# Value projections of the last block with swapped PSUM banks, the short convolution's activation four slots further up, gate rows read out ahead of the splits

## What is computed

```python
def second_block(x, norm_pre, norm_post, w_in, b_if, conv_qk, lambda_qk, norm_a, norm_b, w_a, w_b, w_out):
    h = _rmsnorm(x, norm_pre[l])
    proj = jnp.einsum('bsd,dn->bsn', h, w_in[l])
    qa, ka, va, za, qb, kb, vb, ob, zb, igb, fgb, ga, gb = _split(proj, sizes)
    ...
    oa = _diff_attention(qa, ka, va, lam)
    oa = _rmsnorm(oa, norm_a[l].reshape(H_A, 2 * HEAD_DIM_A)) * (1.0 - lam_init)
    ya = oa.reshape(B, S, W_A) * jax.nn.silu(za)
    qk = jax.nn.silu(_causal_conv(jnp.concatenate([qb, kb], axis=-1), conv_qk[l]))
    ...
    hb = _mlstm(qb_c, kb_c, vb, ig, fg)
    hb = jax.nn.sigmoid(ob.astype(jnp.float32)).reshape(B, S, H_B, HEAD_DIM_B) * hb
    hb = _rmsnorm(hb, norm_b[l].reshape(H_B, HEAD_DIM_B)).astype(x.dtype)
    yb = hb.reshape(B, S, W_B) * jax.nn.silu(zb)
    merged = (jax.nn.sigmoid(ga) * jnp.einsum('bsw,wd->bsd', ya, w_a[l])
              + jax.nn.sigmoid(gb) * jnp.einsum('bsw,wd->bsd', yb, w_b[l]))
    out = jnp.einsum('bsd,de->bse', merged, w_out[l])
    x = x + _rmsnorm(out, norm_post[l])
```

## Time and profile before

| what | value |
|---|---|
| median of 3 executions | 1253.1 us (1253.06 to 1255.51) |
| the profiled execution's own time | 1250.83 us |
| its span, first to last instruction | 1249.6 us |
| TensorE matmul busy | 1220.2 us |
| TensorE weight load busy | 1069.8 us |
| VectorE busy | 881.7 us |
| ScalarE busy | 682.0 us |
| GpSimd busy | 60.7 us |
| granted TensorE clock, mean | 0.996 |
| DMA | 215.46 MB, mean 172 GB/s |

### The profile page before, as it was taken

How to read it: one execution, slowest core, us unless ns; L and a number is a source line. 1 busy time by engine, 2 the same in 40 slices (tenths; PEclk the granted TensorE clock), 3 DMA queues, 4 the chain that set the end, 5 groups by cost and what they waited for, 6 DMA issues and landing times.

```text
span 1249.6 us, 18894 instructions
## 1 busy us (share of the span) xinstructions
PE 1220.2 (98%) x7518; PEld 1069.8 (86%) x7518; DVE 881.7 (71%) x1255; ACT 682.0 (55%) x1033; POOL 60.7 (5%) x89
## 2 busy tenths in 40 slices
PE   7999999989999999999999999999999999899998
PEld 6888888867888888888888887988888899788996
DVE  6686856885787766777766667587776668565875
ACT  5655544533665555555654457556655445555463
POOL 4000100100010000000000122000000000000000
PEclk9999999999999999999999999999999999999999
DMA  8766566771566655666655555156665665646450
GB/s 273 233 206 188 165 189 192 205 183 42 164 195 184 195 172 177 194 192 189 192 183 163 176 190 165 35 152 197 191 194 177 184 188 169 174 118 156 144 174 34
DMA packets 205653, 215.46 MB, mean 172 GB/s; under 512 B 9808, under 2 KB 192592, under 8 KB 205566
## 3 DMA queue, kind: packets, MB, share of 16 engines
q1 hardware_dynamic: 202998, 210.76, 56.8%
q10 hardware_dynamic: 2568, 3.50, 0.9%
HBM read 212.19 MB, written 2.03 MB: 171 GB/s over the span
## 4 chain that ended last, share of the span: by engine, by line
PE 92%; ACT 3%; DVE 2%; issue 1%; DMA 0%; ACTq 0%; POOL 0%; SPq 0%
PE psum L504 90%; ACT whi L1295 1%; DVE wlo L1896 1%; PE psum L668 0%; DMA xn<-in_x 0%; PE psum L953 0%; ACT qn L1599 0%; PE psum L696 0%; ACT L1735 0%; ACTq L1410 0%; DVE small L2333 0%; DVE oa L2543 0%; PE psum L1108 0%; ACT qkc L1699 0%; PE psum L906 0%
## 5 line engine op out<-in xcount | busy, mean ns | idle before, releaser
L504 PE MATMUL psum<-x,whi 128*128 128x512 f32 (+1 forms) x2288 | 696.2, 365 | 5.3 <-ACT whi L1295 2.4
L1896 DVE TENSOR_TENSOR wlo<-raw,whi 128x1024 fp32r<-128x1024 f32 (+2 forms) x403 | 474.3, 1189 | 193.3 <-ACT whi L1295 190.0
L504 PE MATMUL psum<-x,wlo 128*128 128x256 f32 x1960 | 549.3, 280 | 0.8 <-DVE wlo L1896 0.8
L1295 ACT CAST whi<-raw 128x1024 fp32r<-128x1024 f32 (+2 forms) x403 | 406.2, 1022 | 171.6 <-PE psum L504 162.5
L504 PEld LDWEIGHTS psum<-x,whi 128*128 128x128 f32 x2288 | 409.4, 189 | 79.6 <-ACT whi L1295 2.8
L504 PEld LDWEIGHTS psum<-x,wlo 128*128 128x128 f32 x1960 | 371.3, 189 | 1.5 <-DVE wlo L1896 1.3
L504 PE MATMUL psum<-g,whi 128*128 128x512 f32 x704 | 247.7, 396 | 0.0
L504 PE MATMUL psum<-g,wlo 128*128 128x256 f32 x704 | 197.6, 281 | 0.0
L504 PEld LDWEIGHTS psum<-g,whi 128*128 128x128 f32 x704 | 132.3, 188 | 31.8
L504 PE MATMUL psum<-whi,x 128*128 128x512 f32 (+1 forms) x512 | 141.2, 376 | 4.7 <-ACT va L1768 3.3
L504 PEld LDWEIGHTS psum<-g,wlo 128*128 128x128 f32 x704 | 132.2, 188 | 0.0
(11 more groups left out here) (321 smaller groups left out, 851.1 us busy)
## 6 DMA issues: line engine op xcount, KB each, us to landing
raw<-in_ffn_w_gate SPq DMA_DIRECT2D x88, 512.0 KB, 4.5
raw<-in_ffn_w_up SPq DMA_DIRECT2D x88, 512.0 KB, 4.2
raw<-in_ffn_w_down SPq DMA_DIRECT2D x80, 512.0 KB, 3.8
raw<-in_w_in SPq DMA_DIRECT2D x52, 512.0 KB, 3.8
raw<-in_w_o SPq DMA_DIRECT2D x16, 512.0 KB, 4.7
raw<-in_a_w_in SPq DMA_DIRECT2D x14, 512.0 KB, 4.7
raw<-in_w_kv SPq DMA_DIRECT2D x16, 384.0 KB, 3.3
raw<-in_w_mem_kv SPq DMA_DIRECT2D x8, 512.0 KB, 3.7
```

Source lines behind the costliest of these rows:

```text
L504: return pe.matmul(o, l, r, start=start, stop=stop, skip_group_check=True)
L1295: act.copy(held(B.whi[:, i % SPLIT, :], *n), held(B.raw[:, i % RAW, :], *n)).then_inc(*s.hi.now(i))
L1896: dve.tensor_tensor(held(B.wlo[:, i % SPLIT, :], *n), held(B.raw[:, i % RAW, :], *n), held(B.whi[:, i % SPLIT, :], *n).bitcast(F32), ALU.s ...
```

## The change

Three parts, all in the last block.

1. `VB2` is computed into banks 6 and 7 and `VA2` into 4 and 5. TensorE's waits for the first z/o group and for the first transposes of the attention change places with them. On ScalarE the two activations of the short convolution and the one-element exponential stand right behind the read of `vb`, ahead of `use(VA2 + 1)` to `use(VA2 + 3)`, that is, ahead of the splits of z/o slots 1 to 3.
2. In `rest` on VectorE the read of a z/o group's bank 7 stands ahead of `use` in the fourth slot, not behind it.
3. For the third z/o group VectorE reads bank 6 as well; ScalarE's read of it is gone. TensorE's first two column blocks and `z_fn(2)` wait for VectorE.

```diff
@@ -437,7 +437,7 @@
     s.c_act = sig("mix_c_act", ["lam", "ln", ("qk", 0), ("qk", 1)])
     s.v_act = sig("v_rows_act", ["vb", "va"])
     s.ysq = sig("y_squares", [(k, j) for k in ("a", "b") for j in range(8)])
-    s.zo_act = sig("zo_act", range(3))
+    s.zo_act = sig("zo_act", range(2))
     s.z_fn = sig("zo_fn", [1, 0, 2])
     s.expF = sig("mlstm_floor", range(8))
     s.gab_act = sig("gab_sigmoid", range(4))
@@ -483,7 +483,8 @@
     s.cc = sig("conv4", range(4))
     s.c_dve = sig("mix_c_dve", ["g8", "lamsum", "gt", "gmin", "aqk0", "aqk1", "lf", "aqk2", "aqk3", "lam", "vb", "F", "w",
                                 "va", ("zz", 0), ("zz", 2)])
-    s.zo_dve = sig("zo_dve", range(3))
+
+    s.zo_dve = sig("zo_dve", range(4))
     s.gab = sig("gab_cols", range(16))
     s.wd = sig("mlstm_diag", range(8))
     s.floor = sig("mlstm_floor_in", range(8))
@@ -1085,10 +1086,8 @@
                 pe.wait_ge(*s.zo_dve.at(i - 1))
             yield from rows_steps((xh[0], xl[0]), None, 8, ZO2 + 4 * i, 512, [[6], [7]], first=i)
         for c in range(16):
-            if c == 0:
-                pe.wait_ge(*s.zo_act.at(2))
-            elif c == 1:
-                pe.wait_ge(*s.zo_dve.at(2))
+            if c < 2:
+                pe.wait_ge(*s.zo_dve.at(2 + c))
             else:
                 pe.wait_ge(*s.gab.at(c - 2))
             i = GAB2 + c
@@ -1164,13 +1163,13 @@
                 pair(0, 0, AQK2 + 2 * c + e, (6, 7, 2, 3)[c], range(4 * e, 4 * e + 4), e == 0, e == 1)
                 if c == 0 and e == 0:
                     gate_turn()
+        pe.wait_ge(*s.c_dve.at("aqk1"))
+        rows(X0, None, 8, VB2, 512, [[6], [7]])
+        pe.wait_ge(*s.qk.at(2))
+        decay_sums()
         pe.wait_ge(*s.row.at(6))
         pe.wait_ge(*s.c_dve.at("gt"))
-        rows(X0, None, 8, VB2, 512, [[4], [5]])
-        pe.wait_ge(*s.qk.at(2))
-        decay_sums()
-        pe.wait_ge(*s.c_dve.at("aqk1"))
-        rows(X0, None, 8, VA2, 512, [[6], [7]])
+        rows(X0, None, 8, VA2, 512, [[4], [5]])
         rg = rest()
         for i in range(10):
             if i < 8:
@@ -1179,13 +1178,14 @@
                 diff_scores(i)
             if 0 <= i - 1 < 8:
                 if i == 1:
-                    pe.wait_ge(*s.v_act.at("vb"))
+                    pe.wait_ge(*s.v_act.at("va"))
+                    pe.wait_ge(*s.c_dve.at("va"))
                 weights_turn2("d", i - 1)
             if 0 <= i - 2 < 8:
                 values2("d", i - 2, MC.va)
             if i == 0:
-                pe.wait_ge(*s.v_act.at("va"))
-                pe.wait_ge(*s.c_dve.at("va"))
+                pe.wait_ge(*s.v_act.at("vb"))
+                pe.wait_ge(*s.c_dve.at("vb"))
             next(rg)
         for _ in range(3):
             next(rg)
@@ -1703,7 +1703,7 @@
         for i in range(3):
             for k in range(4):
                 use(ZO2 + 4 * i + k)
-                if k == 3:
+                if k == 3 and i < 2:
                     act.wait_ge(*s.zo0.at(i))
                     act.activation(MC.zob[:, i, 0, :], bank[6], ACT.Copy, scale=small[:, 14:15]).then_inc(*s.zo_act.now(i))
                 yield
@@ -1729,8 +1729,9 @@
         act.copy(MC.ptbuf[:, i % 2, 0:nk * 128], bank[4][:, 0:nk * 128]).then_inc(*s.pt_act.now((st, i)))
 
     def z_fn(i, fn):
-        act.wait_ge(*s.zo_act.at(i))
-        act.wait_ge(*s.zo_dve.at(i))
+        if i < 2:
+            act.wait_ge(*s.zo_act.at(i))
+        act.wait_ge(*s.zo_dve.at(i if i < 2 else 3))
         z = flat(MC.zob[:, i])
         act.activation(z, z, fn).then_inc(*s.z_fn.now(i))
 
@@ -1758,14 +1759,14 @@
             use(VB2 + i)
         use(VA2)
         act.wait_ge(*s.used.at(VB2 + 3))
-        act.activation(MC.vb[:, 0, :], bank[4], ACT.Copy, scale=small[:, 14:15]).then_inc(*s.v_act.now("vb"))
-        for i in range(1, 4):
-            use(VA2 + i)
+        act.activation(MC.vb[:, 0, :], bank[6], ACT.Copy, scale=small[:, 14:15]).then_inc(*s.v_act.now("vb"))
         for h in range(2):
             silu_cols(h)
         act.activation(small[0:1, 319:320], B.ones[0:1, 0:1], ACT.Exp)
+        for i in range(1, 4):
+            use(VA2 + i)
         act.wait_ge(*s.used.at(VA2 + 3))
-        act.activation(MC.va[:, 0, :], bank[6], ACT.Copy, scale=small[:, 14:15]).then_inc(*s.v_act.now("va"))
+        act.activation(MC.va[:, 0, :], bank[4], ACT.Copy, scale=small[:, 14:15]).then_inc(*s.v_act.now("va"))
         rg = rest()
         for i in range(10):
             if i < 8:
@@ -2459,11 +2460,15 @@
     def rest():
         for i in range(3):
             for k in range(4):
-                use(ZO2 + 4 * i + k)
                 if k == 3:
+                    if i == 2:
+                        dve.wait_ge(*s.zo0.at(2))
+                        dve.tensor_scalar(MC.zob[:, 2, 0, :], bank[6], small[:, 14:15], None, ALU.mult).then_inc(
+                            *s.zo_dve.now(2))
                     dve.wait_ge(*s.used.at(ZO2 + 4 * i + 3))
                     dve.tensor_scalar(MC.zob[:, i, 1, :], bank[7], small[:, 15:16], None, ALU.mult).then_inc(
-                        *s.zo_dve.now(i))
+                        *s.zo_dve.now(i if i < 2 else 3))
+                use(ZO2 + 4 * i + k)
                 yield
         for c in range(16):
             use(GAB2 + c)
@@ -2615,7 +2620,7 @@
             some(cg, 2)
         some(cg, 100)
         dve.wait_ge(*s.used.at(VB2 + 3))
-        dve.tensor_scalar(MC.vb[:, 1, :], bank[5], small[:, 15:16], None, ALU.mult).then_inc(*s.c_dve.now("vb"))
+        dve.tensor_scalar(MC.vb[:, 1, :], bank[7], small[:, 15:16], None, ALU.mult).then_inc(*s.c_dve.now("vb"))
         use(VA2)
         dve.wait_ge(*s.pe_c.at("F"))
         dve.tensor_copy(Fc, in_pairs(bank[0][:, 0:8])).then_inc(*s.c_dve.now("F"))
@@ -2624,7 +2629,7 @@
         for i in range(1, 4):
             use(VA2 + i)
         dve.wait_ge(*s.used.at(VA2 + 3))
-        dve.tensor_scalar(MC.va[:, 1, :], bank[7], small[:, 15:16], None, ALU.mult).then_inc(*s.c_dve.now("va"))
+        dve.tensor_scalar(MC.va[:, 1, :], bank[5], small[:, 15:16], None, ALU.mult).then_inc(*s.c_dve.now("va"))
         rg = rest()
         dve.wait_ge(*s.c_dve.at("lam"))
         for i in range(10):
```

## The result

The changed kernel took a median of 1245.5 us in five executions (1244.4 to 1247.0), the kernel before 1253.1. The ratio is 0.9934, 95% interval 0.9921 to 0.9946: 8.3 us less by the ratio, with an interval of 6.8 to 9.9. The forecast was 1246.2. The profiled execution took 1244.4 with a span of 1242.9; forecast for its kind, against the profiled execution of before, were 1243.9 and 1242.7.

A forecast was written before the change was run, and what follows sets the result against it. TensorE was taken as the bound, busy 98% at full clock, so only its waits could give time. 3.42 + 0.38 + 1.02 + 2.10 = 6.9 us off the median 1253.1 gave 1246.2 us, range 1244.0 to 1250.0.

The forecast's parts named there:

- The first wait: TensorE between job 0's scores and the z/o rows, waiting for bank reads: z/o rows start 3.42 us earlier.
- The new wait at the turn of job 0: TensorE coming for job 0's weights: weights ready 1.2 us ahead of it, so no new wait there.
- The cover of the splits: ScalarE's splits of z/o slots 1 to 3 behind the moved activation: 6.8 us of delay before TensorE waits.
- The slower rival: Late splits of z/o slots 1 to 3 stop TensorE; 14 us delay for no change, 1256 us at 17; chance 0.03.
- The first group's end: TensorE's wait after the first group of z/o rows goes as VectorE reads bank 7 before its subtraction: 0.38 us.
- The second group's end: After the second group of z/o rows, VectorE's earlier read of bank 7 lets TensorE go on 1.02 us earlier.
- The third group: VectorE alone reads the third z/o group: first column block 2.2 us earlier, third column block 2.10 us earlier.
- Behind it: After the third column block the program is unchanged: nothing given back, nothing more gained.
- The sum: Whole gain in the last block: 3.42 + 0.38 + 1.02 + 2.10 = 6.9 us.
- The upper figure of 7.6: Top of the forecast gain, 7.6 us, if no remainder of TensorE's waits stays in the last block.
- The clock: TensorE's granted clock taken as full throughout the span, from the profile before the change.

The follow-up runs named there:

- the repeat: The changed kernel, unaltered, timed once more on the chip of two other runs: 1245.3 us, ratio 0.9926 (0.9913 to 0.9939) against the kernel before.

## Why the prediction was right, and where not

**The first wait.** Forecast 3.42, measured 3.44. The reason holds: ScalarE's queue, not the bank, carried nearly all of it. The text gave the whole of it to both edits together; apart, the move gains 3.05 and the swap alone 1.3, because the swap alone brings a wait of 1.45 us at the turn of job 0.

**The new wait at the turn of job 0.** Forecast: weights at about 1090.7, TensorE at 1091.85, lead 1.2. Measured: weights at 1090.58 (1090.23 + 0.35), TensorE at 1091.64, lead 1.06.

**The cover of the splits.** Forecast 6.8 us, measured 1.8. This is the step that failed, though it changed nothing in the time. The text priced the subtraction of z/o slot 1 alone; three of them stand in VectorE's queue ahead of the read of bank 5. The slower rival would have decided from 1.8 us of delay on and evened out the gain at 1.8 + 6.6 = 8.4 before the clock's part, not at 14. With the clock's part it was sooner: 6 us of delay gave 162.05 to the end, 0.7 more than before, and a median 1.4 us under that of before; 12 us gave a median 4 us over it.

The rule of the Trainium skill ("ScalarE: Activation LUTs", What ACT_TABLE_LOAD costs), 1.38 us of drain behind a table load, would have mattered here. By an estimate from that figure, two drains are 2.8 us, more than the cover of 1.8, and a wait of 1 us would have stood at job 0. The traces do not have the drain, and no wait stands there. In the runs with added loads a load and its one-element activation take 1.50 us, 1.28 of it the load, and in the changed kernel the activation starts 1.30 after its load did (1077.92, 1079.22).

**The first group's end.** Forecast 0.38, measured 3.97 - 3.44 = 0.53.

**The second group's end.** Forecast 1.02, measured 4.53 - 3.97 = 0.56. The order of read and subtraction did what it should. From job 7's transposes to slot 8 it took 2.09 us before (1123.50, 1125.59) and takes 1.02 now (1119.92, 1120.94), 1.07 less. But the transposes themselves, 3.97 ahead after the first group, are only 3.46 ahead: 0.51 us went there, 0.34 of it as a tag. The text had counted on TensorE coming to this turn with no wait. The round of a job over ScalarE and VectorE takes 4.4 us and starts no earlier than its own work allows; job 5's maxima came 3.1 us earlier, TensorE 4.0. Before, TensorE's waits at the group ends had kept that round ahead (by 0.5 us at job 7: weights at 1123.03, transpose at 1123.50). At the group's end itself it was then ScalarE's read of bank 6, behind its cast (1120.18 + 0.70), that ended last, and no longer VectorE's (1119.95 + 0.74). That a bound of the second rank lies half a microsecond behind the first was not looked for.

**The third group.** Forecast 2.2 at the first column block, 2.10 at the third. Measured 2.13 and 2.06. ScalarE's chain went as worked out: gate activation right behind the cast (1133.87), no wait for VectorE, cast of GAB slot 4 at 1136.35.

**Behind it.** Forecast: nothing given back, nothing more. Measured: 6.59 at the third column block, 6.58 at the end of the span.

**The sum.** 6.9 against 6.6 in the traces: 0.3 too much, the wait at job 7. The upper figure of 7.6 "with no remainder at all" does not come out of the rows: 3.42 + 0.38 + 1.43 + 2.2, each wait with its overlap, is 7.4. Yet the ratio says 8.3 (and 9.3, 7.7 to 10.9, for the repeat). So the forecast of 1246.2 came within 0.7 us with a trace term 0.3 too large and with some 1.7 us that it did not have; that it lay so near is in part luck.

**The clock.** The text took it as full throughout, from the earlier trace rows. A 9 there stands for 90% or more of a slice of 31 us. In that same trace the clock is at half from 271 to 274.8 and from 305 to 308.8 us, as in all the others at about these places. And it took the profiled execution as a plain sample that lay 2.3 us under the median. The runs show a reason for part of that distance. The executions of the kernel before have mean granted clocks from 0.988 to 0.996, and go with them: of 27 in one comparison the two fastest took 1251.3 us, at 0.995, and the seven slowest, 1254.6 to 1256.0, had 0.988 to 0.992. The changed kernel's eleven have 0.993 to 0.996.

Of the six traced kernels that keep the old waits of 3.3 or 2.0 us, with eight such waits in all, three show the clock at half behind one: early reads alone and third group alone behind 3.26, swap alone behind 2.03. It lasted 3.3 to 3.4 us and cost 1.38, 1.54 and 1.47. In the profiled execution of before it did not fall in the block. So such a wait can cost more than its length.

The ratios point to the first wait. Where it is gone or down to 0.3 us, they exceed the traces: by 2.0 us for swap and move (5.5 against 3.52), by 2.2 for the move alone (5.3 against 3.05), by 1.7 and 2.7 for the whole change. Where it stays they agree with the traces within their intervals: 1.8 against 1.18 for the early reads, 1.5 against 2.08 for the third group; so they do for the swap alone, which has 1.45 us in its place (1.8 against 1.3). Each ratio is uncertain by 1 to 2 us. Nor is this the only place. A wait of 2.1 to 2.2 us at about 778 us stands in all thirteen traces, and in three the clock fell within 2 us behind it; behind one of 2.4 at about 12 us it fell in two. The change leaves those as they are, and the slow executions of before may have them too. What is shown is that the clock can fall behind these waits. That their removal makes up the 1.7 us is inferred, since only one execution of before was traced.

## What to carry to other kernels

Where TensorE waits for a bank, look first at what stands ahead of the read in the reader's queue: here moving 4.6 us of table loads and activations out of that place was worth 3.05 us and a free bank 0.4 to 0.5 more. Price the cover of a moved step on the whole path through every in-order queue behind it, with all the pieces that pile up there, not on the one item that moved; and test it by adding delay, which gives the cover as the difference of added time and wait. Do that test with small delays: a long one brings the clock's cost with it. When a first wait goes, see how far the next round (here ScalarE and VectorE) is behind it.

## What the runs showed of the hardware

The granted clock can fall to half behind an idle of TensorE as short as 2.0 us, and did not fall behind the same idle, or one of 3.3 us, in other executions: in the last block it fell behind three of eight such waits, at 778 us behind three of thirteen. In the block it stayed down for 3.3 to 3.4 us and cost 1.4 to 1.5. With idles of 4.2 and 10.2 us it fell within the idle, and the half clock ran on for 5.1 and 5.8 us of matmuls, at a cost of about 3 us each. The Trainium skill ("TensorE: Matmul & The Clock Gate", the table of clock states) has the two levels, 1.2 GHz for an idle engine and 2.4 for a busy one, and these traces agree with the levels: 0.50 and 1.00 of full speed. A wait's price is then its idle tag plus this in a part of the executions, which a single trace may not show.
